# Folding the pool group's linear map and scale into the output weights of an encoder layer

## The reference, cut to what matters

```python
z = h @ w_in                      # columns: pool group (512) | q | k | v
u = z[..., :POOL_W]
# pool_mixer: four channel groups of 128, windows 2, 4, 8, 16
outs.append(win / cnt - uf[:, :, g])                  # centred mean minus the token
m = jnp.stack(outs, axis=2).astype(u.dtype)
y = jnp.einsum('bsgc,gcd->bsgd', m, pool_w)           # a 128x128 map for each group
pool_out = y.reshape(B, S, POOL_W) * pool_scale
# attention of 8 heads over q, k, v gives attn_out
mix = jnp.concatenate([pool_out, attn_out], axis=-1) @ w_out
x = x + rms_norm(mix, ln_mix_post)
```

## Time and profile before

| | |
|---|---|
| three timed runs | 2371.58 us median (2369.41 to 2373.91) |
| span of the profiled execution | 2371.2 us |
| PE busy | 2305.7 us, 97% |
| DVE busy | 1684.8 us, 71% |
| ACT busy | 1038.1 us, 44% |
| POOL busy | 951.7 us, 40% |

### The profile page before, as it was taken

How to read it: one execution, slowest core, us unless ns; L and a number is a source line. 1 busy time by engine, 2 the same in 40 slices (tenths; PEclk the granted TensorE clock), 3 DMA queues, 4 the chain that set the end, 5 groups by cost and what they waited for, 6 DMA issues and landing times.

```text
span 2371.2 us, 29645 instructions
## 1 busy us (share of the span) xinstructions
PE 2305.7 (97%) x10928; PEld 1907.5 (80%) x10928; DVE 1684.8 (71%) x1754; ACT 1038.1 (44%) x1539; POOL 951.7 (40%) x557
## 2 busy tenths in 40 slices
PE   8999999999999989999999999899999999999999
PEld 7888787877778868888887888788788888877877
DVE  5766788888755687676766555888889965575852
ACT  4433788888744453333333222444343333233221
POOL 0000345555423655444443566344456534550210
PEclk9999999999999999999999999999999999999999
DMA  5222233232268884453547867564457587676432
GB/s 198 72 73 97 87 59 74 61 54 59 49 159 246 246 252 161 138 173 122 171 141 262 305 254 263 163 219 163 155 199 260 196 325 265 249 244 236 147 120 75
DMA packets 333550, 402.75 MB, mean 170 GB/s; under 512 B 32736, under 2 KB 236512, under 8 KB 333280
## 3 DMA queue, kind: packets, MB, share of 16 engines
q1 hardware_dynamic: 333408, 400.87, 51.9%
HBM read 259.18 MB, written 137.43 MB: 167 GB/s over the span
## 4 chain that ended last, share of the span: by engine, by line
PE 80%; DVE 8%; DMA 5%; issue 3%; ACT 2%; POOL 1%; SPq 1%; POOLq 0%; DVEq 0%; ACTq 0%
PE ps L1424 46%; PE ps L1213 29%; PE ps L1216 5%; DMA row_scales<-recip 2%; DVE ring L2179 1%; DVE reg L2187 1%; DMA scales<-row_scales 1%; DMA xb<-x_turned 1%; DVE negmax L2083 1%; DMA f_turned<-ev 1%; DVE atb L2097 0%; DVE pt L2125 0%; DVE fhi L2299 0%; DMA ff_forms<-fhi 0%; ACT pt L1529 0%
## 5 line engine op out<-in xcount | busy, mean ns | idle before, releaser
L1424 PE MATMUL ps<-reg,ring 128*128 128x512 f32 x5544 | 1271.0, 391 | 27.0 <-DVE ring L2179 17.7
L1424 PEld LDWEIGHTS ps<-reg,ring 128*128 128x128 f32 x5544 | 1045.5, 189 | 251.2 <-DVE ring L2179 22.0
L1529 ACT ACTIVATE ring<-wraw 128x1024 fp32r<-128x1024 f32 (+2 forms) x152 | 143.7, 946 | 389.5 <-PE ps L1424 389.5
L2179 DVE TENSOR_TENSOR ring<-wraw,ring 128x1024 fp32r<-128x1024 f32 (+2 forms) x152 | 232.2, 1528 | 63.4 <-ACT ring L1529 62.6
L1213 PE MATMUL ps<-win,ht 128*128 128x512 f32 (+1 forms) x1152 | 228.2, 359 | 8.5 <-DVE win L2053 8.3
L1213 PEld LDWEIGHTS ps<-win,ht 128*128 128x128 f32 x1152 | 191.1, 191 | 39.3 <-DVE ht L2010 7.3
L1529 ACT ACTIVATE ring<-ws 128x1024 fp32r<-128x1024 f32 (+2 forms) x114 | 108.0, 947 | 253.3 <-PE ps L1424 236.3
L2179 DVE TENSOR_TENSOR ring<-ws,ring 128x1024 fp32r<-128x1024 f32 (+2 forms) x114 | 175.0, 1535 | 43.2 <-ACT ring L1529 42.6
L2125 DVE TENSOR_TENSOR pt<-ps,pt 128x512 fp32r<-128x512 f32 x256 | 173.6, 685 | 40.5 <-ACT pt L1529 37.6
L1213 PE MATMUL ps<-wout,ct 128*128 128x512 f32 x768 | 180.6, 393 | 2.0 <-DVE wout L2106 1.7
L1529 ACT ACTIVATE pt<-ps 128x512 fp32r<-128x512 f32 x256 | 153.3, 600 | 56.7 <-PE ps L1216 55.9
(11 more groups left out here) (205 smaller groups left out, 2921.4 us busy)
## 6 DMA issues: line engine op xcount, KB each, us to landing
reg<-ff_forms SPq DMA_DIRECT2D x42, 1536.0 KB, 10.0
ff_forms<-fhi SPq DMA_DIRECT2D x88, 512.0 KB, 3.2
wraw<-in_w_gate SPq DMA_DIRECT2D x88, 256.0 KB, 4.2
wraw<-in_w_up SPq DMA_DIRECT2D x88, 256.0 KB, 4.7
ff_forms<-ev SPq DMA_DIRECT2D x44, 512.0 KB, 2.9
wraw<-in_w_down SPq DMA_DIRECT2D x48, 384.0 KB, 5.4
reg<-ff_forms SPq DMA_DIRECT2D x14, 1024.0 KB, 6.8
xt_a<-in_xt SPq DMA_DIRECT2D x16, 512.0 KB, 4.5
```

Of the source, the lines that this page charges most:

```text
L1424: last = nc.tensor.matmul(ps[:, 2 * chain + m, :], ring[:, st % 3, a, m, k * P:(k + 1) * P], reg[:, k, i, e, :], start=OPENS[i] and k == 0 ...
L1529: copy = lambda out, src, **k: nc.scalar.activation(out, src, ACT.Copy, **k)
L2179: V.tensor_tensor(ring_block(u, st, 1), weight_source(u, i), f(ring_block(u, st, 0)), ALU.subtract).then_inc(S["w_split"], 1)
```

## The change

The map and the scale of the pool group are linear and stand directly in front of `w_out`. So the program computes, once, the four products `pool_w[g] * pool_scale` times the rows of `w_out` that belong to group g, and multiplies the plain means by these folded rows in the output projection.

- In the projection stage, PE gets `fold(g)` (six matmuls of 128x512 into banks 5 and 6) at the end of tiles 3 to 6. SP loads the rows of `w_out` (`fold_in`), ACT and DVE split them (`fold_hi`, and a subtraction in DVE's loop), ACT takes the result out (`fold_back`), SP stores it to the memory tensor `out_folded`. The tiles of the fold lie where the second sequence's keys will be, so `turned_rows(8)` waits for the stores.
- `poolw` is now the scaled map: four copies and four subtractions of 128x128 in place of one of 128x512, with `pool_w` laid out transposed in memory beforehand, and `pscale` loaded with it.
- In attention, `pooled(h)` goes from PE and ACT, and the split into `mt_hl` from POOL. `windows(h)` writes the means straight to `plb`, and `pooled_out` waits for POOL (`m_ready`) and no longer for ACT.
- `out_strip(0)` to `out_strip(3)` read `out_folded` instead of `w_out`.
- Some semaphores of the last stage are shared with the new ones, with raised thresholds.

```diff
@@ SP
             def out_strip(k):
-                sp.dma_start(out_place(k), w_out[k * P:(k + 1) * P, :]).then_inc(S[f"strip_in{k}"], 16)
+                rows = wf_d[k] if k < NPOOL else w_out[k * P:(k + 1) * P, :]
+                sp.dma_start(out_place(k), rows).then_inc(S[f"strip_in{k}"], 16)
...
+            def fold_in(g):
+
+                sp.wait_ge(S["strip_split"], KT)
+                sp.wait_ge(S["fold_split"], g)
+                sp.dma_start(fold_raw[:], w_out[g * P:(g + 1) * P, :]).then_inc(S["fold_in"], 16)
...
                 turned_in(n)
                 sp.wait_ge(S["x_sum"], n)
                 rows_in(n)
+                if 3 <= n < 3 + NPOOL:
+                    fold_in(n - 3)
+                if 5 <= n < 5 + NPOOL:
+                    sp.wait_ge(S["fold_out"], n - 4)
+                    sp.dma_start(wf_d[n - 5], fold_out[:]).then_inc(S["fold_st"], 16)
...
             def pooled_out(job):
-                sp.wait_ge(S["misc_free"], MISC[("pool", job)] + 1)
+                sp.wait_ge(S["m_ready"], job + 1)
@@ POOL, windows(job)
-                go(nc.gpsimd.tensor_tensor(m[:, 8:520], s[:, 8:520],
-                                           u[:, PAD + t0:PAD + t0 + 512], ALU.subtract))
-                if job >= 1:
-                    pool.wait_ge(S["misc_done"], MISC[("pool", job - 1)] + 1)
-                    alone(pool)
-                go(nc.gpsimd.tensor_copy(mt_hl[:, 0, :], m[:, 8:520]))
-                nc.gpsimd.tensor_tensor(mt_hl[:, 1, :], m[:, 8:520], mt_hl[:, 0, :].bitcast(F32),
-                                        ALU.subtract).then_inc(S["m_ready"], 1)
...
+                pool.wait_ge(*at_least(f"pl_out{hf}", 16 * (job // 2)))
+                alone(pool)
+                nc.gpsimd.tensor_tensor(plb[:, hf], s[:, 8:520],
+                                        u[:, PAD + t0:PAD + t0 + 512], ALU.subtract).then_inc(S["m_ready"], 1)
@@ PE, turn_rows(n) and the loop of the projection
                 pe.wait_ge(S["u_stored"], n)
+                if 3 <= n < 3 + NPOOL:
+                    pe.wait_ge(S["fold_out"], n - 2)
...
+            def fold(g):
+
+                pe.wait_ge(S["fold_split"], g + 1)
+                pe.wait_ge(S["u_stored"], g + 3)
+                pe.wait_ge(S["k_stored"], g + 3)
+                for c in range(2):
+                    for m, (a, b) in enumerate(((0, 0), (0, 1), (1, 0))):
+                        last = mm(ps[:, 5 + c, :], poolw[:, a, g, :], fold_hl[:, b, c * 512:(c + 1) * 512],
+                                  m == 0, m == 2)
+                last.then_inc(S["fold_done"], 1)
...
                 columns(n, Q)
                 if n == 2:
                     turn_rows(1)
+                if 3 <= n < 3 + NPOOL:
+                    fold(n - 3)
@@ PE, attention
-            def pooled(job):
-                misc(("pool", job))
-                pe.wait_ge(S["m_ready"], job + 1)
-                for m, (a, b) in enumerate(((0, 0), (0, 1), (1, 0))):
-                    last = mm(ps[:, 7, :], poolw[:, a, job % NH // 2, :], mt_hl[:, b, :], m == 0, m == 2)
-                last.then_inc(S["misc_done"], 1)
...
-                if u == 7:
-                    pooled(h)
@@ ACT, turned_rows(n) and the loop of the projection
+                if n == NT:
+                    act.wait_ge(S["fold_st"], 16 * NPOOL)
                 act.wait_ge(S["u_turned"], n + 1)
...
+            def fold_hi(g):
+
+                act.wait_ge(S["fold_in"], 16 * (g + 1))
+                act.wait_ge(S["fold_done"], g)
+                copy(fold_hl[:, 0], fold_raw[:]).then_inc(S["fold_hi"], 1)
+
+            def fold_back(g):
+
+                act.wait_ge(S["fold_done"], g + 1)
+                act.wait_ge(S["fold_st"], 16 * g)
+                copy(fold_out[:], pair(5)).then_inc(S["fold_out"], 1)
...
                 q_root(n)
+                if 3 <= n < 3 + NPOOL:
+                    fold_back(n - 3)
+                if 2 <= n < 2 + NPOOL:
+                    fold_hi(n - 2)
...
-            def pooled(job):
-                half, k = job % 2, job % NH // 2
-                misc_wait(("pool", job))
-                act.wait_ge(*at_least(f"pl_out{half}", 16 * (job // 2)))
-                copy(plb[:, half], ps[:, 7, :], scale=pscale[:, k:k + 1]).then_inc(S["misc_free"], 1)
@@ DVE, the loop of the projection
                 q_rows(n)
+                if 2 <= n < 2 + NPOOL:
+                    dve.wait_ge(S["fold_hi"], n - 1)
+                    V.tensor_tensor(fold_hl[:, 1], fold_raw[:], f(fold_hl[:, 0]), ALU.subtract)\
+                        .then_inc(S["fold_split"], 1)
```

More of the change, by code:

```diff
@@ L175 @@
 NSTEP = NSEQ * NH * NT
-NCONST = 9
+NCONST = 8
 def encoder_layer(nc, x, xt, p, ident_d, cos_d, sin_d, edge_d, g_mix_pre, g_mix_post, w_in, pool_w,
@@ L188, in encoder_layer @@
     q_d = nc.dram_tensor("query_rows", (NT, P, NH * HD), F32, kind="Internal").ap()
+    wf_d = nc.dram_tensor("out_folded", (NPOOL, P, D), F32, kind="Internal").ap()
     r_d = nc.dram_tensor("row_scales", (2 * NSEQ * NH, 4, P), F32, kind="Internal").ap()
@@ L235, in encoder_layer @@
         s_k.close()
+        s_f = ExitStack()
+        sb(s_f, "keys_first", [P, NKV * 2 * SEQ])
+        fold_raw = sb(s_f, "fold_raw", [P, D])
+        fold_hl = sb(s_f, "fold_hl", [P, 2, D], F32R)
+        fold_out = sb(s_f, "fold_out", [P, D])
+        s_f.close()
         keys = sb(one, "keys", [P, NSEQ, NKV, 2, SEQ], F32R)
@@ L281, in encoder_layer @@
         pt = sb(s_c, "pt", [P, 2, 2, KT, 4 * P], F32R)
-        mt_hl = sb(s_c, "mt_hl", [P, 2, 512], F32R)
+        sb(s_c, "to_atb", [P, 2 * 512])
         atb = sb(s_c, "atb", [P, 2, 512])
@@ L558, in _ @@
                 sp.wait_ge(S[f"q_st{b}"], 16 * (NT // 2))
+            sp.wait_ge(S["fold_st"], 16 * NPOOL)
             for k in range(6):
@@ L1015, in windows @@
                 grp, hf = job % NH // 2, job % 2
+                if job:
+                    pool.wait_ge(S["m_ready"], job)
+                    alone(pool)
                 u = chan[:, grp, :]
@@ L1046, in windows @@
                 go(nc.gpsimd.tensor_scalar(s[:, 8:520], s[:, 8:520], 1.0 / w, None, ALU.mult))
-                go(nc.gpsimd.tensor_tensor(m[:, 8:520], s[:, 8:520],
-                                           u[:, PAD + t0:PAD + t0 + 512], ALU.subtract))
-                if job >= 1:
-                    pool.wait_ge(S["misc_done"], MISC[("pool", job - 1)] + 1)
-                    alone(pool)
-                go(nc.gpsimd.tensor_copy(mt_hl[:, 0, :], m[:, 8:520]))
-                nc.gpsimd.tensor_tensor(mt_hl[:, 1, :], m[:, 8:520], mt_hl[:, 0, :].bitcast(F32),
-                                        ALU.subtract).then_inc(S["m_ready"], 1)
+                if job == 0:
+                    for b in range(2):
+                        pool.wait_ge(S[f"u_st{b}"], 16 * (NT // 2))
+                        alone(pool)
+                        pool.wait_ge(S[f"q_st{b}"], 16 * (NT // 2))
+                        alone(pool)
+                pool.wait_ge(*at_least(f"pl_out{hf}", 16 * (job // 2)))
+                alone(pool)
+                nc.gpsimd.tensor_tensor(plb[:, hf], s[:, 8:520],
+                                        u[:, PAD + t0:PAD + t0 + 512], ALU.subtract).then_inc(S["m_ready"], 1)
             def add_parts(hc):
@@ L1490, in embed_tile @@
                                       k == 1 and r == 2)
-                last.then_inc(S["proj_done"], 1)
+                last.then_inc(on("proj_done"), 1)
             pe.wait_ge(S["a_end"], NU)
@@ L1614, in _ @@
                 strip(k)
-            act.wait_ge(S["pw_raw"], 16)
-            copy(poolw[:, 0].rearrange("p g n -> p (g n)"), qtok[:].rearrange("p h d -> p (h d)"))\
-                .then_inc(S["early_hi"], 1)
+            act.wait_ge(S["pw_raw"], 32)
+            raw = qtok[:].rearrange("p h d -> p (h d)")
+            for g in range(NPOOL):
+                last = copy(poolw[:, 0, g], raw[:, g * P:(g + 1) * P], scale=pscale[:, g:g + 1])
+            last.then_inc(S["early_hi"], 1)
             square(0)
@@ L1909, in tokens_hi @@
             def tokens_hi(s):
[L1911 removed]
+                act.wait_ge(*at_least("p_in", 16 * (s + 1)))
                 if s:
[L1913 removed]
+                    act.wait_ge(*at_least("proj_done", KT))
                 else:
@@ L1917, in tokens_hi @@
                     last = copy(pturn[:, k, 0], praw_t[:, k])
-                last.then_inc(S["pp_hi"], 1)
+                last.then_inc(on("pp_hi"), 1)
             def second_hi(k):
@@ L1944, in _ @@
                         nc.scalar.activation(sig[:, m % 2, t * CH:(t + 1) * CH], ps[:, 2 * (m % 2) + t, :],
-                                             ACT.Sigmoid, bias=bgate[:, n:n + 1]).then_inc(S["sig_done"], 1)
+                                             ACT.Sigmoid, bias=bgate[:, n:n + 1]).then_inc(on("sig_done"), 1)
                     break
@@ L2059, in _ @@
             dve.wait_ge(S["early_hi"], 2)
```

(13 more changed lines are left out.)

52 lines of the change are left out of this document (27 added, 25 removed).

## The result

The changed kernel takes 2384.3 us (median of 20 runs, 2375.99 to 2391.52) where the kernel before, on the same chip, takes 2373.15 us (20 runs, 2365.86 to 2384.31). The ratio is 1.0045, 95% interval 1.0033 to 1.0058: slower by 10.7 us (7.8 to 13.8). The forecast was +3.2 us, 2374.8, with a range up to 2379; the result lies outside it.

The account below looks back on a forecast made before the run. The prediction took PE to bound the projection, with DVE right behind PE in attention. Projection +7.7, attention products -2.5 and GpSimd -2.0 gave +3.2 on 2371.2: 2374.4 span, 2374.8 us with 0.4 added; range 2366 to 2379.

Parts of the forecast that it names:

- the attention term, -4.5: Attention: products removed from PE save 2.5 us and GpSimd's lighter load 2.0 us.
- Fold products, +5.5: Projection, end of tiles 3 to 6: 24 added 128x512 products at 0.228 us each cost 5.5 us.
- Fold gap, +2.2: Projection, before the first fold: PE stands from 69.7 to 71.9 until ACT's `keys` copy frees bank 6.
- Rival 1, the clock: PE's clock falls after the fold gap and head 12's gap: both +6.6 us, 2378.2; one 2376.5; chance 0.29.
- Products out of attention, -2.5: Attention: 48 products leave PE; odd heads 1 to 11 give 1.8 us, head 0 0.7, the others nothing.
- Rival 2 (-10.9): PE bounds attention everywhere, so all 10.9 us of removed products come off: total -5.2 us, 2366.4; chance 0.15.
- GpSimd, -2.0: Attention: without Pool's `mt_hl` split, DVE's `o_scale` meets Pool less often, saving 2.0 us; bounds 0 and -4.4.
- the landings of the scales: Attention, heads 12 and 13: `o_scale` waits for a DMA issued before the removed product, so those heads gain 0.
- The stages behind attention differ by more than 1 us: Stages after attention: a difference of more than 1 us there was named as a sign that the prediction is wrong.
- the relief would come back whole: Attention: by the skill's port-lock rule, the whole 2.9 us of `o_scale` slowed by Pool's split returns, sum 0.9 lower.

Follow-up runs that it names:

- The attention part alone: Only the attention edits against before, no fold in the projection, pool map and scale left out: 1.0008 (+1.9 us), repeated 1.0002 (+0.5 us).
- the fold part: The folds put into the projection, attention as in before, so the map is applied twice: 1.0039 (+9.2 us), on another chip 1.0040, against before.
- late fold: The changed kernel with all four folds one tile later (tiles 4 to 7): 1.0010 and, on another chip, 1.0014 times before.
- the pair without trip: After and before, each with row scales through memory for the first four half heads alone, the others reusing those: 0.9998 and 0.9973 times before.
- the kernel with products back: After with three unused products per head given back to PE where the pool group's stood: 1.0048 (1.0028 to 1.0068) times before.
- no fold: Before with only the attention edits, no fold in the projection, pool map and scale left out: 1.0008, repeated 1.0002.
- Before without trip: Before with row scales through memory for the first four half heads alone, the rest scaled with those: 0.9973 (0.9961 to 0.9984).

## Why the prediction was wrong, step by step

The step that failed is the attention term, -4.5: it was put into the sum as if each piece taken off an engine there came off the whole time. The attention part alone measured +1.9 and +0.5 us, 5 to 6 us more than that. A second term, the clock, stood at nothing in the sum and cost 1.5 us behind the gap and about 1 at the start of attention. Term by term:

- *Fold products, +5.5.* Right: 4 x 1.37 = 5.5.
- *Fold gap, +2.2.* Right: 2.3 by the turns on either side, with PE idle for 1.98 to 2.02 us in all ten executions, `keys` ending just before and no gap at folds 1 to 3, as forecast.
- *Rival 1, the clock.* It came, in seven of ten executions, and costs 1.5 us there; the loss that I took from the earlier trace rows was 1.7. I gave it 0.29 because the gap is shorter than the 2.39 us one of the earlier trace rows; at 2.0 us it is the more likely case. This explains the 9.4 us of the fold part, where 7.7 was forecast.
- *A term that wasn't in the sum.* Where the attention stage begins, PE waits for `qh`, and the clock is low again. From the first `qh` turn to the third, before takes 11.4 and 11.0 us in its two profiles, after 12.4 in both. The granted clock is 0.51 in after's 262 to 272, 0.72 in before's 251 to 261. Other kernels show 11, 11.4 or 12.5 to 12.7 us, and a late fold is among the longest, so this too falls one way or the other: about +1 here.
- *Products out of attention, -2.5.* Right in the pair without trip: -0.72 for head 0, some -0.3 for each odd head, next to nothing for even heads, 3.7 with GpSimd's 0.9 in it. Rival 2 (-10.9) is refuted by the kernel with products back: its undisturbed heads grew by only 0.7 (head 0, to 22.3) and 0.3 (odd ones, to 23.4).
- *GpSimd, -2.0.* Right in kind: the meetings with `o_scale` count in full, and fewer of them are worth 0.9 us in the pair without trip and some 1.6 in the mean of the profiles with it. The 4.4 us in all that it was taken from were one execution's.
- *The sum of the two, -4.5, on the whole time.* Wrong, as said. The forecast priced the landings of the scales at nothing, but for the heads where they showed in one profile. With the trip in place heads 0 to 12 take 313.6 and 312.2 us in before, 318.7 and 310.9 in after, 314.1 and 316.9 in no fold, 307.0 and 306.8 in late fold; without it 308.3 and 305.6. After, no fold and late fold have the same attention code, and they differ by more than the change was to bring.
- *"The stages behind attention differ by more than 1 us" would prove it wrong, I wrote.* They do. In most profiles of the new kernels PE waits there for the last weights. Timeline of after:

```profile
678.00 14.46 PE L1243 MATMUL ps<-wout,ct 128*128 128x512 f32 x54 [6.10 <-DVE wout L2161]
```

Before stood 1.70 us there. In the chain of waits of after, 14.13 us of `ws<-in_w_out` lie ahead of it: the second of two loads that SP issues from 660.36 on, behind the last round trips. The last of the two took 7.3 and 7.9 us in before's profiles and 10.8 to 15.2 in all fifteen of kernels with any part of the change and the trip; why isn't shown. It costs little by itself, because before is late at another place, in head 13 (26.7 and 30.6 us). From the first turn of head 13 to the end of the output projection before takes 267.2 and 272.6 us, after 267.4 and 268.1. Before without trip has no such gap in its timeline:

```profile
639.58 22.67 PE L1217 MATMUL ps<-wout,ct 128*128 128x512 f32 x96 [0.26 <-issue]
```

The sum with what was measured is 5.5 + 2.3 + 1.5 + 1.0 - 3.7 = +6.6 us. The pair without trip, which leaves out the landings of the scales, differs by 5.9 us. The two comparisons of after and before gave 6.2 and 10.7. The 4 us between 6.6 and 10.7, and the 4 to 6 us by which "no fold" misses its -3.7, lie by these readings mainly in long heads, which go with SP's round trips. They are also there in before (heads of 26.4 to 30.6 us), and one or two profiles per kernel can't say whether the change makes them more frequent. This stays open.

A rule of the Trainium skill explains in part why even heads had no slack. "VectorE: DVE Perf Modes", section "Two Vector instructions with no wait between them", gives a model by which an instruction whose input or output starts in another quadrant (group of 32 partitions) of the same memory than the last one's is held until every earlier one has finished. In even heads `o_scale` works on rows 64 to 127, the instructions around it start at row 0. The trace of before agrees. Its timeline in head 2, and then in head 3:

```profile
315.42 0.69 DVE L2097 TENSOR_TENSOR atb<-atb,scales 64x512 f32<-64x512 f32 x1
316.14 1.22 DVE L2083 TENSOR_REDUCE negmax<-ps 128x1 f32<-128x1024 f32 x1
...
350.66 0.67 DVE L2097 TENSOR_TENSOR atb<-atb,scales 64x512 f32<-64x512 f32 x1
351.26 1.21 DVE L2083 TENSOR_REDUCE negmax<-ps 128x1 f32<-128x1024 f32 x1
```

From start to start 0.72 us there, 0.60 here. By the Trainium skill's "SBUF — State Buffer", section "🔬 SBUF: two separate sides", weighed in the prediction, the loser of a meeting with GpSimd is blocked, and the relief would come back whole. The trace agrees in the single meeting: 1.0 us longer `o_scale`, 1.0 us longer head.

No kernel with the whole computation beats before. The best new one is the late fold, at 1.0010 and 1.0014.

## What to carry to other kernels

Work moved off one engine pays only where that engine ends the wait: read the interval between two of its instructions with and without the piece, head by head, as was done here for the products. Even then it pays in the whole time only if nothing later swallows it; in a stage that hangs on DMA round trips, take the trip out of both kernels and compare those, and take more than one profile before a mean is put into a sum. A new gap in a dense product stage costs its length and can cost the clock besides, here 2.3 us and, in seven of ten executions, 1.5 more; an order that avoids it (here one tile later) gives both back.

## What the runs showed of the hardware

- The same gap of 2.0 us before the same products let the granted clock fall in seven executions of ten (0.63 and 0.76 against 1.00 over four us).
- SP, waiting for a write of 2 KB in elements of four bytes, could go on only 15.6 us after its issue, and what waited for a 128 KB transfer issued 2.2 us behind it in the same queue began 13.8 us after that one's issue.
- A VectorE multiplication of 64x512 (0.67 to 0.69 us alone) took up to 1.82 us beside a GpSimd instruction, and the head that held one of 1.69 us was 1.0 us longer.
- The first long block of products began at 9.30 us in one execution of before and at 10.62 in another.
- Taking 0.5 us off each of VectorE's 32 `o_scale` didn't change the time beyond its interval (1.0041 against 1.0043 and 1.0048 on the same chip).
